# Two chained transformer blocks on one core: the last output tiles, the norms, the first weight tiles, the pooling stage and the output worked in two halves of 256 tokens

## The reference

```python
def first_block(x, ...):
    h = _rms_norm(x, norm_mix[l])
    ...
    x = x + y @ w_out[l]
    x = x + _conv_ffn(_rms_norm(x, norm_ffn[l]), ffn_up[l], ffn_conv[l], ffn_down[l])

def second_block(x, c, ...):
    for i in range(DEPTH_2):
        h = modulate(rms_norm(x, norm_g[i, 0]), sh0, sc0)
        x = x + 0.5 * g0 * swiglu(h, ffn_w_gu[i, 0], ffn_w_down[i, 0])
        h = modulate(rms_norm(x, norm_g[i, 1]), sh1, sc1)
        y = pool_mixer(h, ...) if i == 0 else diff_attention(h, ...)
        x = x + g1 * y
        h = modulate(rms_norm(x, norm_g[i, 2]), sh2, sc2)
        x = x + 0.5 * g2 * swiglu(h, ffn_w_gu[i, 1], ffn_w_down[i, 1])
    return rms_norm(x, final_g)

def rms_norm(x, g):
    y = xf * lax.rsqrt(jnp.mean(xf * xf, axis=-1, keepdims=True) + EPS)
```

## Time and profile before

| | |
|---|---|
| time, median of 3 runs (lowest to highest) | 2855.18 us (2854.01 to 2857.14) |
| the profiled execution: its span, first to last instruction | 2868.0 us |
| PE busy, of the span | 97% |
| share of PE in the chain that ended last | 91% |
| DVE, ACT, POOL busy | 50%, 34%, 8% |
| mean granted clock of PE | 0.986 |

### The profile page before, as it was taken

How to read it: one execution, slowest core, us unless ns; L and a number is a source line. 1 busy time by engine, 2 the same in 40 slices (tenths; PEclk the granted TensorE clock), 3 DMA queues, 4 the chain that set the end, 5 groups by cost and what they waited for, 6 DMA issues and landing times.

```text
span 2868.0 us, 40754 instructions
## 1 busy us (share of the span) xinstructions
PE 2783.2 (97%) x16211; PEld 2249.2 (78%) x16211; DVE 1428.6 (50%) x2059; ACT 979.6 (34%) x1530; POOL 241.9 (8%) x318
## 2 busy tenths in 40 slices
PE   8999888999999999999989999999999999999998
PEld 7855777887887878888878888788887866788887
DVE  4588643666776455555443332433324876433322
ACT  3355443333332232222342222322223265422222
POOL 1000110112000111001110000100002300100000
PEclk8899999999999999999999999999999999999999
DMA  6331001673332655566323333233333310233332
GB/s 234 115 99 59 3 3 32 218 229 118 102 93 87 204 152 195 186 199 197 100 68 95 95 95 98 88 95 95 92 101 97 108 37 23 77 100 95 93 94 70
DMA packets 89844, 311.07 MB, mean 108 GB/s; under 512 B 11632, under 2 KB 12400, under 8 KB 89584
## 3 DMA queue, kind: packets, MB, share of 16 engines
q1 hardware_dynamic: 66928, 232.62, 26.0%
q0 software_dynamic: 22784, 76.56, 8.7%
HBM read 305.99 MB, written 2.10 MB: 107 GB/s over the span
## 4 chain that ended last, share of the span: by engine, by line
PE 91%; DVE 4%; ACT 3%; issue 1%; POOL 1%; DMA 1%; SPq 0%; DVEq 0%; ACTq 0%; POOLq 0%
PE psum L1924 24%; PE psum L1926 24%; PE psum L1925 24%; PE psum L2101 1%; PE psum L2103 1%; PE psum L2102 1%; PE psum L2612 1%; PE psum L2601 1%; PE psum L1999 1%; PE psum L1995 1%; PE psum L1996 1%; PE psum L2303 1%; PE psum L2076 1%; PE psum L2392 1%; PE psum L2273 1%
## 5 line engine op out<-in xcount | busy, mean ns | idle before, releaser
L1144 DVE TENSOR_TENSOR w_lo<-stage,w_hi 128x1024 fp32r<-128x1024 f32 (+2 forms) x441 | 518.3, 1175 | 827.4 <-ACT w_hi L655 827.2
L655 ACT ACTIVATE w_hi<-stage 128x1024 fp32r<-128x1024 f32 (+2 forms) x441 | 449.7, 1020 | 1206.1 <-PE psum L1926 1171.7
L1924 PE MATMUL psum<-h_hi,w_hi 128*128 128x512 f32 (+1 forms) x2024 | 792.7, 392 | 3.3 <-DVE w_lo L1144 2.3
L1925 PE MATMUL psum<-h_lo,w_hi 128*128 128x512 f32 (+1 forms) x2024 | 790.9, 391 | 0.0
L1926 PE MATMUL psum<-h_hi,w_lo 128*128 128x512 f32 (+1 forms) x2024 | 790.5, 391 | 0.0
L1924 PEld LDWEIGHTS psum<-h_hi,w_hi 128*128 128x128 f32 (+1 forms) x2024 | 381.1, 188 | 86.7 <-DVE w_lo L1144 4.4
L1926 PEld LDWEIGHTS psum<-h_hi,w_lo 128*128 128x128 f32 (+1 forms) x2024 | 381.0, 188 | 80.2
L1925 PEld LDWEIGHTS psum<-h_lo,w_hi 128*128 128x128 f32 (+1 forms) x2024 | 381.1, 188 | 79.6
L1924 PE MATMUL psum<-hid_hi,w_hi 128*128 128x512 f32 x880 | 344.0, 391 | 6.5 <-DVE hid L1234 6.5
L1926 PE MATMUL psum<-hid_hi,w_lo 128*128 128x512 f32 x880 | 343.4, 390 | 0.0
L1925 PE MATMUL psum<-hid_lo,w_hi 128*128 128x512 f32 x880 | 343.2, 390 | 0.0
(11 more groups left out here) (440 smaller groups left out, 3023.0 us busy)
## 6 DMA issues: line engine op xcount, KB each, us to landing
stage<-in_up SPq DMA_DIRECT2D x220, 512.0 KB, 3.6
mod_w<-in_mod_w POOLq DMA_DIRECT2D x144, 512.0 KB, 4.3
stage<-in_down SPq DMA_DIRECT2D x80, 448.0 KB, 3.3
stage<-in_down SPq DMA_DIRECT2D x40, 512.0 KB, 3.5
stage<-in_w_in SPq DMA_DIRECT2D x24, 512.0 KB, 3.6
stage<-in_w_qkv SPq DMA_DIRECT2D x24, 512.0 KB, 3.6
stage<-in_w_merge SPq DMA_DIRECT2D x16, 512.0 KB, 4.5
turned_n<-in_cmp_w SPq DMA_DIRECT2D x1, 4096.0 KB, 13.1
```

Source lines behind the costliest of these rows:

```text
L655: act.activation(w_hi[:, c % 2, 0:kt * cols], stage[:, c % NSTAGE, 0:kt * cols], ACT.Copy).then_inc(hi_done, 1)
L1144: dve.tensor_tensor(w_lo[:, c % 2, 0:kt * cols], stage[:, c % NSTAGE, 0:kt * cols], w_hi[:, c % 2, 0:kt * cols].bitcast(F32), ALU.subtract ...
L1924: pe.matmul(dst, wh[:, n], a_hi[:, k], start=start and n == 0, stop=False)
L1925: pe.matmul(dst, wh[:, n], a_lo[:, k], start=False, stop=False)
```

## The change

The 512 tokens are worked as two halves of 256 (`HALVES`) around each crossing, so that the first half's norm can start while PE still works on the second half.

- The last output tile of each `down` (the last two of `mix_out` and `attn_out`: `LATE`) is computed by `half_product`, the second half in another bank (`last_bank`), and the sums of squares and the spreading of the first half stand between its matmuls.
- `cross` on ACT and DVE takes the place of `root`/`round_h` and `norm`; everything between the last output tile and the first two units is done per half with operations on 256 columns.
- `half_units` takes the place of `first_units` (except at norm 0). `keep_busy` is gone.
- The pooling stage runs per half; its weights come as 2 tiles in place of 4, and POOL sums the squares per half (`gather_half`).
- The output is stored by four DMAs of 512 KB, two per half.
- The Silu table is loaded after the norm's rounding and not before; two small vector computations (`mod_vectors`) move into `down0` and `down2`.

```diff
+HS = S // 2
+HALVES = (slice(0, HS), slice(HS, S))
+LATE = {n: (6, 7) if n in (1, 7) else (7,) for n in range(1, 9)}
...
@@ tensor
-            def keep_busy(count):
...
+            def half_product(c, k_tiles, acts, dst, half, start, stop, between=None):
+                kt, cols = shape_of(c)
+                if half == 0:
+                    pe.wait_ge(lo_done, c + 1)
...
+                for n, k in enumerate(k_tiles):
+                    pe.matmul(dst[:, at], wh[:, n], acts[0][:, k, at], start=start and n == 0, stop=False)
+                    pe.matmul(dst[:, at], wh[:, n], acts[1][:, k, at], start=False, stop=False)
+                    m = pe.matmul(dst[:, at], wl[:, n], acts[0][:, k, at], start=False, stop=stop and n == kt - 1)
+                    if n == 4 and between:
+                        between()
...
+            def half_units(s, n_norm):
+                for half in range(2):
+                    tokens = HALVES[half]
+                    for k in range(KD + LAG):
+                        if half == 0 and k == 4:
+                            sum_late(n_norm, 1)
+                        if half == 0 and k == 7:
+                            spread_rstd(n_norm, 1)
+                        for e, at in ((0, k), (1, k - LAG)):
...
             def down(f, n_norm):
...
+                half_product(c, ranges[0], acts, first, 0, True, False)
+                half_product(c, ranges[0], acts, second, 1, True, False).then_inc(unit_done, 1)
+                half_product(c + 1, ranges[1], acts, first, 0, False, False)
+                sum_early(n_norm)
+                half_product(c + 2, ranges[2], acts, first, 0, False, True).then_inc(half_done, 1)
+                half_product(c + 1, ranges[1], acts, second, 1, False, False,
+                             lambda: sum_late(n_norm, 0)).then_inc(unit_done, 1)
+                spread_rstd(n_norm, 0)
+                half_product(c + 2, ranges[2], acts, second, 1, False, True).then_inc(unit_done, 1)
...
@@ tensor, pooling stage
+                for half in range(2):
+                    for g in range(4):
...
+                            if half and g % 2 == 0:
+                                if (tt, g) == (3, 0):
+                                    pe.wait_ge(z_act, 1)
...
+                pe.wait_ge(acc_done, adds_before(4) + 12)
+                sums_of(sq_sum, 1, False, False)
                 up(2, 4)
...
@@ scalar
+            def cross(n_norm, shift, c, silu=True):
+                for k in LATE[n_norm]:
+                    square(n_norm, k, 0)
+                root(n_norm, 0)
+                hi(c)
+                round_half(n_norm, shift, 0, 0, 2)
+                hi(c + 1)
+                round_half(n_norm, shift, 0, 2, 4)
+                for k in LATE[n_norm]:
+                    square(n_norm, k, 1)
+                round_half(n_norm, shift, 0, 4, 6)
+                root(n_norm, 1)
+                round_half(n_norm, shift, 0, 6, KD)
+                round_half(n_norm, shift, 1, 0, KD)
+                if silu:
                     warm(ACT.Silu)
...
@@ vector
+            def cross(s, n_norm, gate, scale, shift, c):
+                for n in late:
+                    add_half(s, n_norm, n, 0, gate)
+                invert(n_norm, 0)
+                scaled_half(n_norm, scale, 0, 0)
+                scaled_half(n_norm, scale, 0, 1)
+                if len(late) == 2:
+                    add_half(s, n_norm, late[0], 1, gate)
+                lo(c)
+                low_half(n_norm, shift, 0, 0)
+                scaled_half(n_norm, scale, 0, 2)
+                scaled_half(n_norm, scale, 0, 3)
+                add_half(s, n_norm, KD - 1, 1, gate)
+                low_half(n_norm, shift, 0, 2)
+                lo(c + 1)
...
+                second_half(n_norm, scale, shift)
```

683 lines of the change are left out of this document (430 added, 253 removed).

## The result

The changed kernel takes 2877.4 us (median of 6 executions, 2868.7 to 2891.9) against 2855.2 for the kernel before beside it (6 executions, 2853.4 to 2864.9): a ratio of 1.0081, 95% interval 1.0059 to 1.0103. So it is slower, by 22 us at the medians, and the forecast of 2864.9 had 9.7. Run again later beside others it took 2869.95 (11 executions), ratio 1.0057 (1.0037 to 1.0077). All 17 executions together have a median of 2877.1, a mean of 2876.6 and a mean granted clock of 0.985; 115 executions of the kernel before beside the later runs have 2859.9 and 0.989. The profiled execution took 2877.47 us with a span of 2875.8.

A forecast was written before the change was run, and what follows sets the result against it. PE, busy 97% of the span, was taken as the bound, so only matmul time and PE's waits count. Crossings 7.6, pooling stage 2.3 plus clock 3.7, tail -3.9 gave +9.7 on 2855.2: 2864.9 us, range 2852 to 2874.

The forecast's parts named there:

- Pooling stage: Pooling stage walked in halves at full clock: 61.9 us against 59.57, +2.3 (bounds +0.3 and +4.2), clock cost on top.
- clock +3.7: Pooling stage: half-rate clock behind PE's waits of 3.4 and 5.7 us loses 1.7 and 2.0 us.
- the clock falls at crossings too: Rival: short waits in each crossing's first half lower the clock, 1.2 to 1.7 us each; +7, 2872 us; chance 0.20 including high bounds.
- Prices: Assumed half-width operation times: ACT 0.40 without and 0.50 with bias, DVE 0.47, POOL 0.72, half matmul 0.120 us.
- Steps 1 to 4 of the walk: Norm 5's first half: sums, spreading done at 15.5 (4.2 us earlier), scaling and roundings; PE waits 2.6 us in all.
- step 4: Norm 5: roundings of k = 2, 3 queue behind ACT's `hi` of unit 1's weights; PE waits 1.0 us at k = 2.
- Step 5: Norm 5's second half: DVE gets the spreading at 26.2, POOL's last low part ends at 33.4; PE waits 1.2 us more.
- Step 6, the new wait for `w_lo`: Norm 5: unit 0 ends at 33.9; the shorter lag of unit 1 makes PE wait 1.33 us for unit 2's weights.
- Step 7: Norm 5: unit 2 starts at 36.3; terms sum to 10.5 us against 8.93 lost before, +1.6.
- Sum over the crossings: Crossings of norms 1, 2, 5, 6, 7 lengthen by +1.1, +1.6, +1.6, +1.5, +1.8, together +7.6 us (bounds 3.1 and 11.7).
- Tail: Kernel's end: halved copies gain nothing (last still 12.6 us after ideal), smaller stores gain; -3.9 us, between -2 and -4.5.

The follow-up runs named there:

- after_lag8: The changed kernel with unit 1 of the second half wholly behind unit 0 (8 k-tiles, not 3): 2879.0 us, ratio to the kernel before 1.0071.
- after_busy3: The changed kernel with unread matmuls ahead of PE's waits at crossings and in the pooling stage, including the low-part wait after k = 2: 2860.4 us, ratio to before 1.0017.

## Why the prediction was wrong

The direction and most of the sum were right; the forecast of 2864.9 was 12.5 us too low, and the measured 2877.4 lies above the range's end, 2874. The step that failed is the last term under "Pooling stage", **clock +3.7**, and with it the place given to the rival "the clock falls at crossings too", which had 0.20 and was what happened, together with longer falls in the pooling stage than any I had priced.

Rows of the changed kernel at the crossing of norm 5: PE, DVE, POOL, and the sizes of the half operations on ACT, DVE and POOL.

```profile
1826.62 0.61 PE L2149 MATMUL psum<-cst,rstd 128*128 128x128 f32 x4
...
1831.35 0.38 PE L2233 MATMUL psum<-h_hi,w_hi 128*128 128x256 f32 x1 [0.64 <-ACT h_hi L771]
...
1833.59 0.39 PE L2237 MATMUL psum<-h_lo,w_hi 128*128 128x256 f32 x1 [1.09 <-POOL h_lo L620]
...
1837.26 0.61 PE L2149 MATMUL psum<-cst,rstd 128*128 128x128 f32 x4
...
1847.86 0.50 PE L2118 MATMUL psum<-h_hi,w_hi 128*128 128x512 f32 x1 [1.09 <-DVE w_lo L1246]
```

```profile
1846.59 1.22 DVE L1246 TENSOR_TENSOR w_lo<-stage,w_hi 128x1024 fp32r<-128x1024 f32 x1 [2.78 <-ACT w_hi L730]
```

```profile
1832.17 1.36 POOL L620 TENSOR_TENSOR h_lo<-rexp,h_hi 128x256 fp32r<-128x256 f32 x1 [1.91 <-ACT rexp L773]
```

```profile
L771 ACT ACTIVATE h_hi<-rexp,modv 128x256 fp32r<-128x256 f32 x8 | 3.7, 501 | 0.9 <-DVE rexp L1282 0.6
L1282 DVE SCALAR_TENSOR_TENSOR rexp<-xT,scales,psum 128x256 f32<-128x256 f32 x8 | 3.5, 475 | 0.0
L1289 DVE SCALAR_TENSOR_TENSOR h_lo<-rexp,modv,h_hi 128x256 fp32r<-128x256 f32 x4 | 1.9, 485 | 1.0 <-ACT h_hi L771 0.9
L620 POOL TENSOR_TENSOR h_lo<-norm_t,h_hi 128x256 fp32r<-128x256 f32 x4 | 3.2, 799 | 16.2 <-ACT norm_t L773 16.2
```

- **Prices.** Right: ACT 0.501 (0.50), DVE 0.475 and 0.485 (0.47), POOL 0.73 to 0.74 in most rows (0.72). POOL's mean of 0.80 holds one row of 0.99. Its longest row, the 1.36 above, lies beside DVE's `w_lo` of 1831.73, which kept its 1.22: there it was POOL that stretched and not DVE. In the pooling stage DVE has longer rows beside POOL too (0.65 and 0.84).
- **Steps 1 to 4 of the walk.** The tile's first matmul is at 1811.98. The spreading was to end at 15.5 and ended at 15.3. The wait at k = 2 was to be 1.0 and is 0.64, for ACT's rounding behind `hi` as in step 4. The longest wait, 1.09, comes one k-tile later, at k = 3, for POOL's low part, the row of 1.36: the walk had no stretch for POOL there.
- **Step 5.** DVE gets the second half's spread at 25.9 (26.2). POOL's last low part ends at 1844.90, at 32.9 (33.4).
- **Step 6, the new wait for `w_lo`.** 1.33 forecast; 1.04 to 1.11 at all six places. Its reading as a loss of its own is refuted by after_lag8, but the sum took it as the end of a chain and stays.
- **Step 7.** The third unit was to start at 36.3 and starts at 35.9 in the traces with the clock at 1.00.
- **Sum over the crossings, at full clock.** 7.6 forecast (1.1, 1.6, 1.6, 1.5, 1.8); 7.7 measured (2.4, 1.1, 1.1, 1.2, 1.9). Norm 1 was under-priced and norms 2, 5 and 6 over-priced, so that the sum fits this well is partly luck. At norm 1 PE waits 0.82 us for POOL's last addition to the sum of squares of the tiles before (`rexp`, L594), which I had not seen.
- **Pooling stage.** 61.9 from the end of the tile's products, so 76.9 from its start; measured 75.9 and 76.8 at full clock (77.6 with the further filler of after_busy3). The +2.3 compared this with a stage that had 17 us at half clock; against the old stage at full clock, 70.0, the halves cost 5.9 to 6.8. With both kernels at full clock the change is thus worth 7.7 + 5.9 to 6.8 - 5.7 = +7.9 to +8.8. The waits:

```profile
1431.87 0.38 PE L2790 MATMUL psum<-w_hi,h_hi 128*128 128x256 f32 x1 [2.98 <-ACT z_tok L1129]
...
1441.59 1.76 PE L2811 MATMUL psum<-band,z_tok 128*128 128x136 f32 x13 [2.46 <-DVE xT L1938]
...
1459.21 1.01 PE L2126 MATMUL psum<-cst,rexp 128*128 128x1 f32 x4 [5.69 <-POOL rexp L603]
```

  3.4, 2.5 and 5.7 forecast; 2.98, 2.46 and 5.69 found. The third is POOL's queue as argued, an addition behind two low parts:

```profile
1454.78 0.73 POOL L620 TENSOR_TENSOR h_lo<-norm_t,h_hi 128x256 fp32r<-128x256 f32 x1 [2.70 <-ACT norm_t L773]
1455.46 0.73 POOL L603 TENSOR_TENSOR rexp<-rexp,norm_t 128x256 f32<-128x256 f32 x1
1457.57 0.73 POOL L620 TENSOR_TENSOR h_lo<-rexp,h_hi 128x256 fp32r<-128x256 f32 x1 [1.39 <-ACT rexp L773]
1458.25 0.91 POOL L603 TENSOR_TENSOR rexp<-rexp,norm_t 128x256 f32<-128x256 f32 x1
```

- **Tail.** -3.9 forecast, -5.7 measured. "Twice as many copies of half the size gain nothing" was wrong by 2.1: the last copy ends 10.5 us after the ideal end of the products, not 12.6. Before, each pair of copies waited a round trip through two `y_out` buffers; with four, ten copies run back to back; what each of this and the early start gives was not measured apart. From the last copy to the end 3.3 us (2.8 to 3.0).

```profile
2868.61 3.92 ACT L1225 ACTIVATE out_tok<-psum 128x256 f32<-128x256 f32 x10 [0.67 <-PE psum L2978]
```

- **The clock.** With the changed kernel at full clock and the kernel before as it is, the sum is 7.7 + 1.4 to 2.2 - 5.7 = +3.4 to +4.2, against 7.6 + 2.3 - 3.9 = +6.0 forecast. The mean difference of all executions is 16.7, so the clock adds about 13 where I had 3.7; the fillers take 13 out again. In the two profiles of the change it is 5.4 and 8.6 us at the crossings (norm 1 1.0 and 2.5, norm 2 1.0 and 1.0, norm 5 0 and 2.5, norm 6 1.0 and 0, norm 7 2.3 and 2.6, against the lengths of after_busy3) and 1.3 and 7.3 in the pooling stage (against 76.8). The change puts waits of 0.4 to 1.1 us close together and takes out `keep_busy`, and puts dense products where the clock is then low. I had listed those waits, and priced the fall at 1.2 to 1.7 each; the error was to want a wait of 1.8 us or more, the only kind behind which I had seen a fall in the trace of before, before believing in it. And that in the pooling stage the half clock can come to 24 to 34 us, partly over dense work (10.20 of 10.20 us busy in one of its pieces), no row of before had shown.

The median of 22 us holds some luck besides, this time bad: of the first six executions of the kernel before one was in its upper group, where a third is usual, and the changed kernel's second series, 2869.95, would have been inside the range. Profile against profile, both with the 27 us in the first mixer, the forecast was 2877.7 and the span 2875.8; but that execution had only 1.3 of the 7.3 us that half clock cost in the other's pooling stage. What brings the long stretches, in the first mixer and in the pooling stage, in some executions and not in others, was not found.

## What to carry to other kernels

Splitting a norm in halves shortens the way to the first product, but pays for it with operations of a fixed cost on every engine, and the chain behind the last piece (here the last low part and the next weights) still sets the end: walk to that end before counting the early start as gained. Before removing filler work or spreading one long wait into many short ones, ask whether dense matmuls will stand behind them: a lower clock costs little where PE waits for others anyway, and a third of its length or more where it doesn't. Where a program's executions fall into groups, compare stages of traces at equal clock first, then the medians.

## What the runs showed of the hardware that I had not expected

- Among waits of 0.4 to 1.1 us, close together, the granted clock fell to 0.50 for 3.4 or 6.8 us, at four of five crossings in one profile and four in another (norm 5 stayed at 1.00 in the one, norm 6 in the other). With work that nobody reads in those waits it was 1.00 at all five crossings of after_busy3, and the mean clock of 12 executions 0.993 in place of 0.985.
- Half clock can last 27.3 us with PE busy throughout (first mixer), and comes by execution: the same pooling stage had 10.2, 23.9 and 34.1 us of it in three profiles (PE busy in 25.6 of a stretch of 30.7 in after_lag8), and none in three with fillers.
- Twice the time at half clock (123 us against 66) can cost about 5 us, under a tenth of the time added, where PE waits for other engines in it.
- A matmul of 256 columns of plain float32 is two instructions and takes 0.44 us, one of a product of the same width 0.12.
